# The token mixer's steps moved between the products of the input projection

## The chip, the cores and the metric

One core of one Trainium2 chip runs one program. The metric is the device time of an execution in microseconds (us); the median of three runs is shown. A core has TensorE (PE; its weight loads are PEld), VectorE (DVE), ScalarE (ACT), GpSimd (POOL) and SyncE (SP), each with an instruction queue of its own that runs in order; they wait for each other with semaphores. Sixteen DMA engines move data for all queues.

## The reference

One inference step of a two-layer diffusion backbone for 384 tokens of width 1024, in three tiles of 128: tile 0 is the new context request, tiles 1 and 2 are the 256 latent tokens (a grid of 4 rows x 64). Each layer, cut to what matters:

```python
mod = ada_modulation(cvec, w_ada[l], b_ada[l])            # silu(c) @ w_ada, 6 x 1024 columns
h = rms_norm(x, norm_g[l, 0]) * (1 + sc_m) + sh_m
q, k, v, u, vm, bg, cg, hx = split_projection(h @ w_in)   # 512,512,512,256,256,256,256,256 columns
o_att = attend(q, k, v)          # context: dense softmax; latents: masked window + bias, and cached context keys
vm = rms_norm(gelu(vm), g_v)
o_mlp = gelu(u) * (einsum('hpq,bcqhd->bcphd', w_s, vc) + b_s)      # chunks of 128 tokens
o_conv = bg * sum(pad(cg * hx)[:, j:j + n] * w_conv[:, j] for j in range(3))
y = concatenate([o_att, o_mlp, o_conv]) @ w_out
x = x + gt_m * rms_norm(y, norm_g[l, 1])
# then a second norm with modulation, and SwiGLU: dense in layer 0, top-2 of 8 experts in layer 1
```

## The kernel before

All weights come from memory in chunks of 1 MB (two transfers of 512 KB) through a ring `raw` of six slots, in the order of a table `STREAM`. SP issues chunk n when TensorE has finished chunk n - 6 (`s_pe`). A projection runs in split precision: ScalarE copies a chunk rounded to `whi` (three buffers, line 574), VectorE writes the remainder over the ring slot as `wlo` (line 805), and TensorE makes three products per piece (`three`, lines 1134 to 1136). The helper `upto(n)` stands wherever ScalarE or VectorE should have split the stream up to chunk n; what follows it on that queue waits.

The input projection `win` has eleven chunks per layer: columns in blocks of 512, two chunks (the two halves of the 1024 inputs) per block, in the order q, k, v, u with vm, B with C, and one 256-wide chunk for h. Per chunk and token tile there are 12 products of 512 columns (24 of 256 in the last). Sums stand in PSUM banks 2t + b%2, and ScalarE evacuates them to `pr` (line 713). Modulation weights are not split: TensorE multiplies them raw (`ada`, line 1173, 16 products for a group of two chunks), after each of eight input chunks (`ADA_IN_WIN`) one group; VectorE adds the bias row that POOL loads (`brow`), and for some groups TensorE turns the row into columns (`ada_turn`, line 1158).

Behind the projection stands `mixer`, on each engine as a block of its own: transposes of q, k and the cached keys (lines 1249, 1253), the gating products (1260), row shifts for the convolution as products with a shift matrix (1274), and then twelve units, each a pair of heads of one tile: scores (1291 to 1294), VectorE's scaling, bias and maximum (`soft`, 1016 to 1026), ScalarE's exponential (744), transposes of the weights (1303), ScalarE's copy (753), products with the values (1317), VectorE's division (1033). The convolution (999 to 1004) sits on VectorE between the second and third unit. Last, eight column tiles of `pr` are transposed (1336) and split into `xhi` and `xlo`, and the output projection `wout` (four chunks q) begins. POOL prepares the position bias in two steps: 8 small loads (line 485), one transfer of all rows to memory in a repeated form (`rpb_pad`, line 487), and 16 transfers back (`bias`, line 497).

## Time and profile before

| | us |
|---|---|
| median of three runs (1877.98 to 1895.23) | 1886.65 |
| profiled execution, its own time | 1877.55 |
| its span, first to last instruction | 1875.7 |
| PE busy | 1695.2 (90%) |
| DVE busy | 1093.5 (58%) |
| ACT busy | 928.3 (49%) |
| mean granted TensorE clock | 0.942 |

Busy time of PE is the time in which a product is under way; products are pipelined, so it says little of the rate. The clock is the granted share of full speed, 1.00 for 2.4 GHz and 0.50 for 1.2 GHz. In order of time the program is: start with the first modulation groups and the norm (to 55.6 us), layer 0 with its mixer and dense channel part, layer 1 from about 603 us with its mixer, and the experts from about 905 us to the end.

### The profile page before, as it was taken

To read this page: it belongs to the slowest core of one execution; us is meant where nothing else is said; L and a number is where in the kernel's file an instruction comes from. 1 tells how busy PE (TensorE), PEld (TensorE's weight loads), DVE (VectorE), ACT (ScalarE), POOL (GpSimd) and SP (SyncE) were. 2 spreads that over 40 slices of the span, in tenths; PEclk is the share of its full clock that TensorE was granted. 3 is DMA by queue.
4 is the path that set the end of the run, shared out by engine and by line. 5 is a ranking of instruction groups with operands and counts; after the bars stand their busy time and mean duration, and the time that the engine had idled before them with its cause. 6 is when DMAs were issued, how large, how long until landed. Compare 5 with 4: busy or idle time off the path is not lost.

```text
span 1875.7 us, 20363 instructions
## 1 busy us (share of the span) xinstructions
PE 1695.2 (90%) x7938; PEld 1336.3 (71%) x7938; DVE 1093.5 (58%) x1214; ACT 928.3 (49%) x1137; POOL 177.5 (9%) x189
## 2 busy tenths in 40 slices
PE   4988787999999888788599999999999999999994
PEld 1656675888877656676488788778887777787772
DVE  1423635343323423543399888889888966666653
ACT  2314335332313324245377777777777755545541
POOL 3220000000000230000202011020202020010001
PEclk9998887999999889887699999999999999999996
DMA  9795012343354796002399999999999986566643
GB/s 331 228 318 189 23 46 68 113 135 113 134 213 169 191 307 243 23 24 68 136 356 367 352 376 349 372 350 378 350 381 350 374 261 204 207 222 215 218 160 114
DMA packets 296572, 423.19 MB, mean 226 GB/s; under 512 B 22116, under 2 KB 226944, under 8 KB 296464
## 3 DMA queue, kind: packets, MB, share of 16 engines
q1 hardware_dynamic: 281504, 394.85, 62.1%
q0 software_dynamic: 13952, 24.29, 4.8%
q10 hardware_dynamic: 1008, 2.62, 0.4%
q8 instruction: 67, 1.10, 0.2%
q14 instruction: 41, 0.34, 0.1%
HBM read 418.56 MB, written 21.99 MB: 235 GB/s over the span
## 4 chain that ended last, share of the span: by engine, by line
PE 81%; DVE 6%; DMA 5%; ACT 3%; issue 3%; SPq 1%; POOL 0%; POOLq 0%; DVEq 0%; ACTq 0%
PE ps L1134 22%; PE ps L1136 21%; PE ps L1135 21%; PE ps L1140 3%; PE ps L1141 3%; DMA raw<-in_w_in_dram 2%; PE ps L1173 2%; PE ps L1401 1%; SPq L399 1%; PE ps L1479 1%; DMA raw<-in_w_moe_gu_dram 1%; PE ps L1317 1%; PE ps L1198 1%; PE ps L1158 1%; DMA raw<-in_w_ada_dram 1%
## 5 line engine op out<-in xcount | busy, mean ns | idle before, releaser
L805 DVE TENSOR_TENSOR wlo<-raw,whi 128x2048 fp32r<-128x2048 f32 x327 | 746.8, 2291 | 369.2 <-ACT whi L574 368.6
L574 ACT ACTIVATE whi<-raw 128x2048 fp32r<-128x2048 f32 x327 | 625.9, 1917 | 377.2 <-DMA raw<-in_w_in_dram 122.3
L1134 PE MATMUL ps<-whi,xhi 128*128 128x512 f32 (+1 forms) x1352 | 543.4, 402 | 42.0 <-issue 19.6
L1135 PE MATMUL ps<-wlo,xhi 128*128 128x512 f32 (+1 forms) x1352 | 528.0, 391 | 0.0
L1136 PE MATMUL ps<-whi,xlo 128*128 128x512 f32 (+1 forms) x1352 | 527.9, 390 | 0.0
L1134 PEld LDWEIGHTS ps<-whi,xhi 128*128 128x128 f32 x1352 | 258.9, 192 | 114.3 <-DVE wlo L805 31.0
L1136 PEld LDWEIGHTS ps<-whi,xlo 128*128 128x128 f32 x1352 | 258.2, 191 | 53.9
L1135 PEld LDWEIGHTS ps<-wlo,xhi 128*128 128x128 f32 x1352 | 259.3, 192 | 48.1 <-issue 0.5
L1134 PE MATMUL ps<-whi,hhi 128*128 128x512 f32 x484 | 196.8, 407 | 0.4 <-DVE pg L910 0.4
L1136 PE MATMUL ps<-whi,hlo 128*128 128x512 f32 x484 | 190.2, 393 | 0.0
L1135 PE MATMUL ps<-wlo,hhi 128*128 128x512 f32 x484 | 189.1, 391 | 0.0
L1136 PEld LDWEIGHTS ps<-whi,hlo 128*128 128x128 f32 x484 | 90.9, 188 | 19.9
L1134 PEld LDWEIGHTS ps<-whi,hhi 128*128 128x128 f32 x484 | 91.0, 188 | 19.0 <-DVE pg L910 1.3
L1135 PEld LDWEIGHTS ps<-wlo,hhi 128*128 128x128 f32 x484 | 91.2, 188 | 17.3 <-issue 0.2
L538 POOL DMA_INDIRECT hx<-h_rows,lidx x24 | 49.7, 2069 | 523.0 <-PE ps L1479 431.0
L659 ACT ACTIVATE pg<-ps 128x256 f32<-128x256 f32 x121 | 43.6, 380 | 100.4 <-PE ps L1401 91.2
L908 DVE TENSOR_TENSOR pg<-pg,ps 128x256 f32<-128x256 f32 x121 | 48.5, 416 | 70.7 <-ACT pg L659 60.1
L551 POOL DMA_INDIRECT y_rows<-f,lidx x24 | 45.8, 1910 | 324.7 <-ACT f L698 318.0
L672 ACT ACTIVATE xhi<-ps 128x384 fp32r<-128x384 f32 x64 | 31.4, 491 | 86.0 <-PE ps L1479 85.4
L1140 PE MATMUL ps<-whi,xhi 128*128 128x512 f32 x176 | 68.6, 390 | 2.0 <-DVE xhi L929 2.0
L1173 PE MATMUL ps<-raw,cS 128*32 128x512 f32 x384 | 53.8, 675 | 18.3 <-DMA raw<-in_w_ada_dram 17.5
L1141 PE MATMUL ps<-wlo,xhi 128*128 128x512 f32 x176 | 68.7, 390 | 0.0
(211 smaller groups left out, 1389.0 us busy)
## 6 DMA issues: line engine op xcount, KB each, us to landing
raw<-in_w_moe_gu_dram SPq DMA_DIRECT2D x352, 512.0 KB, 6.0
raw<-in_w_moe_d_dram SPq DMA_DIRECT2D x176, 512.0 KB, 6.2
raw<-in_w_ada_dram SPq DMA_DIRECT2D x96, 512.0 KB, 5.5
raw<-in_w_in_dram SPq DMA_DIRECT2D x44, 512.0 KB, 5.7
raw<-in_w_ffn_gu_dram SPq DMA_DIRECT2D x44, 512.0 KB, 4.3
raw<-in_w_ffn_d_dram SPq DMA_DIRECT2D x22, 512.0 KB, 6.5
raw<-in_w_out_dram SPq DMA_DIRECT2D x16, 512.0 KB, 4.4
rpb_pad<-pad POOLq DMA_DIRECT2D x2, 1778.0 KB, 17.9
```

What stands on the lines that cost most here:

```text
L538: pool.indirect_dma_start(out=hx[:, i, :], out_offset=None, in_=h_rows[:, :], in_offset=bass.IndirectOffsetOnAxis(ap=lidx[:, e, i:i + 1], ...
L551: pool.indirect_dma_start(out=y_rows[:, :], out_offset=bass.IndirectOffsetOnAxis(ap=lidx[:, e, i:i + 1], axis=0), in_=f[:, i, :], in_offse ...
L574: act.activation(whi[m % SPL][:, :], raw[n % RING][:, :], ACT.Copy).then_inc(s_hi, 1)
L659: ins = act.activation(pg[:, t, :], ps[:, 2 * t + b % 2, 0:256], ACT.Silu)
L805: dve.tensor_tensor(wlo[n % RING][:, :], raw[n % RING][:, :], whi[NTH[n] % SPL][:, :].bitcast(F32), ALU.subtract).then_inc(s_lo, 1)
L908: ins = dve.tensor_tensor(pg[:, t, :], pg[:, t, :], ps[:, 2 * t + b % 2, 256:512], ALU.mult)
L1134: pe.matmul(out, a_hi, w_hi, start=start, stop=False)
L1135: pe.matmul(out, a_hi, w_lo, start=False, stop=False)
L1136: return pe.matmul(out, a_lo, w_hi, start=False, stop=stop)
L1140: pe.matmul(out, a, w_hi, start=start, stop=False)
L1141: return pe.matmul(out, a, w_lo, start=False, stop=stop)
L1173: ins = pe.matmul(ps[32 * k:32 * k + 32, 6, :], cS[:, 4 * h + k, :], w[:, k, :], start=(h == 0), stop=(h == 1))
```

## The change

The input chunks come in another order (`WIN_SEQ`): u with vm first, then q, k, v, then h, and B with C last. In the following, position 0 to 10 is a chunk's place in that order, and a slot is one token tile of a chunk, so that a chunk is three slots. The modulation groups stand two together behind positions 2 to 5 (`ADA_AFTER`) instead of one behind each of eight chunks. Each token tile has one PSUM bank (t) for its sums, used by all blocks in turn. The mixer's steps are called from inside `win` on every engine, by tables that name the slot: transposes in positions 5 and 6, scores from position 7 on, a unit's transposes two slots behind its score and its value products three behind. The gating part runs from position 1 to 4. The context units come first and share one value step. The last value step, six of the eight column tiles and the convolution move into `wout`. The row shifts are no longer products: POOL copies z shifted by one row to `zp` and `zn`. POOL also issues its small loads, the bias rows and their detour ahead of the fifth modulation row. Buffers move accordingly.

```diff
-ADA_IN_WIN = {w: HEAD + w - 1 for w in range(1, 1 + ADA_B - HEAD)}
+WIN_SEQ = [6, 7, 0, 1, 2, 3, 4, 5, 10, 8, 9]
+ADA_AFTER = {2 + p: [HEAD + 2 * p, HEAD + 2 * p + 1] for p in range((ADA_B - HEAD) // 2)}
...
-        for w in range(N_WIN):
+        for p, w in enumerate(WIN_SEQ):
             out.append(("win", l, w))
-            if w in ADA_IN_WIN:
-                out += [("ada", l, 2 * ADA_IN_WIN[w] + h) for h in range(2)]
+            for i in ADA_AFTER.get(p, []):
+                out += [("ada", l, 2 * i + h) for h in range(2)]
...
-        UNITS = [(t, h) for t in (1, 2, 0) for h in range(0, NH, 2)]
...
+        UNITS = [(0, h) for h in range(0, NH, 2)] + [(t, h) for h in range(0, NH, 2) for t in (1, 2)]
         NU = len(UNITS)
+        N_OWN = NH // 2
+        QK = [("q", 0), ("q", 1), ("q", 2), ("q", 3), ("c", 0), ("k", 0), ("k", 1), ("k", 2), ("k", 3)]
+        QK_AT = {-3: [0, 1], -2: [2, 3], 0: [4], 1: [5, 6], 2: [7, 8]}
+        SCORE_AT = [3, 3, 4, 4] + list(range(5, 13))
+        OWN_AT = 7
+        MIXED_AT = {13: [0, 1]}
+        MIXED_BANK = [5, 6, 6, 7, 6, 7, 6, 7]
...
+        def slot(p, t):
+            return NT * (p - 6) + t
+        def units_at(j, lag):
+            return [u for u in range(NU) if SCORE_AT[u] + lag == j]
...
@@ POOL
+            def shift_rows(l):
+                pool.wait_ge(s_sc, NU * (l + 1))
...
+                pool.wait_ge(s_z, l + 1)
+                pool.dma_start(zp[1:P, :, :], z[0:P - 1, :, :]).then_inc(s_zs, 16)
+                pool.dma_start(zn[0:P - 1, :, :], z[1:P, :, :]).then_inc(s_zs, 16)
+                pool.wait_ge(s_zs, 64 * l + 32)
+                pool.dma_start(zp[0:1, 2, :], z[P - 1:P, 1, :]).then_inc(s_zs, 16)
+                pool.dma_start(zn[P - 1:P, 1, :], z[0:1, 2, :]).then_inc(s_zs, 16)
...
+                pool.dma_start(ws[:, :, :], w_s[l].rearrange("h p q -> p h q")).then_inc(s_ld[l][1], 16)
+                pool.dma_start(bs[:, :], b_s[l].rearrange("h p -> p h")).then_inc(s_ld[l][2], 16)
+                chain(pool.memset(pad[:, :], NEG))
+                for h in range(NH):
+                    pool.dma_start(pad[7 * h:7 * h + 7, 48:79], rpb[l, h, 4:11, :]).then_inc(s_pad, 16)
+                pool.dma_start(ck[:, :], cache_k[0, l].rearrange("p h d -> p (h d)")).then_inc(s_ld[l][4], 16)
+                pool.dma_start(cv[:, :], cache_v[0, l].rearrange("p h d -> p (h d)")).then_inc(s_ld[l][5], 16)
+                pool.wait_ge(s_pad, (16 * NH + 16) * (l + 1) - 16)
+                pool.dma_start(rpb_pad[l], pad[0:56, :].rearrange("p (a k) -> p a k", a=1).to_broadcast([56, GW, 127])
...
+                pool.dma_start(wcb[:, :, :].rearrange("p c j -> p (c j)"),
...
+                pool.wait_ge(s_tr, KT * (2 * l + 1))
+                clear_brow(l, HEAD)
                 norm_row(l, 1)
                 brow(l, 4)
                 brow(l, 5)
...
@@ ScalarE, in win(l)
+                for p, w in enumerate(WIN_SEQ):
+                    n, b = PLACE["win", l, w], w // 2
+                    last = w % 2 == 1 or w == 10
...
                     for t in range(NT):
...
+                        j = slot(p, t)
+                        if t == 0:
+                            upto(HALVED[NTH[n] + (1 if 1 <= p <= 5 else 2)])
+                        if last:
+                            if t < NT - 1:
+                                act.wait_ge(s_win, 2 * WIN_B * l + 2 * k + t + 1)
+                            else:
+                                act.wait_ge(s_pe, n + 1)
+                            act.activation(pr[:, t, 512 * b:512 * b + width], ps[:, t, 0:width], ACT.Copy
+                                           ).then_inc(s_pr, 1)
+                        for i in QK_AT.get(j, []):
+                            if i % 2 == 0:
+                                turned_qk(l, i)
+                        for u in units_at(j, 2):
+                            pt_copy(l, u)
+                        for kt in MIXED_AT.get(j, []):
+                            mixed(l, kt)
+                        for u in units_at(j, 0):
+                            exp(l, u)
+                    if p == 1:
...
+                        act.activation(pr[:, :, OU:OU + 512], pr[:, :, OU:OU + 512], ACT.Gelu_apprx_tanh
+                                       ).then_inc(s_gel, 1)
+                        act.wait_ge(s_gel, l + 1)
+                        act.wait_ge(s_pad, (16 * NH + 16) * (l + 1))
+                        for t in range(NT):
+                            rms(5 * l + 1, t, pr[:, t, OVM:OVM + D_CM], sq[:, :], D_CM)
...
+                upto(PLACE["wout", l, 2])
+                for kt in (2, 3, 4, 5):
+                    mixed(l, kt)
+                upto(PLACE["wout", l, 3])
+                for kt in (6, 7):
+                    mixed(l, kt)
...
@@ VectorE
+            def win(l):
+                for p, w in enumerate(WIN_SEQ):
+                    n = PLACE["win", l, w]
+                    for t in range(NT):
+                        j = slot(p, t)
+                        for i in QK_AT.get(j, []):
+                            if i % 2 == 1:
+                                turned_qk(l, i)
+                        for u in units_at(j, 0):
+                            if u == N_OWN:
+                                masked_bias(l)
+                            soft(l, u)
+                        if j == OWN_AT:
+                            own_out(l)
+                        for u in units_at(j, 3):
+                            if u >= N_OWN:
+                                out(l, u)
+                        for kt in MIXED_AT.get(j, []):
+                            mixed(l, kt)
+                        if j == 1:
+                            mod_columns(l, 1)
+                        if t == (1 if p > 5 else 0):
+                            upto(HALVED[NTH[n] + (1 if 1 <= p <= 5 else 2)])
+                    if p == 2:
+                        gate_values(l)
+                    if p == 4:
+                        gated_units(l)
+                    for i in ADA_AFTER.get(p, []):
+                        ada(l, i)
+                    if p == 2:
+                        dve.wait_ge(s_wsp, l + 1)
+                        dve.tensor_copy(wsT[:, :, :].rearrange("p a n -> p (a n)"), ps[:, 3, :]).then_inc(s_wst, 1)
                 dve.wait_ge(s_pr, NT * WIN_B * (l + 1))
                 dve.tensor_tensor(z[:, :, :], pr[:, :, OC:OC + D_CV], pr[:, :, OH:OH + D_CV], ALU.mult
                                   ).then_inc(s_z, 1)
...
+                upto(PLACE["wout", l, 2])
+                out(l, NU - 1)
+                for kt in (2, 3, 4, 5):
+                    mixed(l, kt)
+                convolve(l)
+                upto(PLACE["wout", l, 3])
+                for kt in (6, 7):
+                    mixed(l, kt)
...
@@ TensorE
+            def win(l):
+                k = 0
+                for p, w in enumerate(WIN_SEQ):
+                    b, h = (w // 2, w % 2) if w < 10 else (5, 0)
...
+                    n = PLACE["win", l, w]
+                    pe.wait_ge(s_lo, NTH[n] + 1)
...
                     for t in range(NT):
...
+                        if k and h == 0:
+                            pe.wait_ge(s_pr, NT * WIN_B * l + NT * (k - 1) + t + 1)
+                        for i in range(kk):
+                            kt = 4 * h + i
+                            if p < 2 and t == 0:
+                                pe.wait_ge(s_xlo, KT * 2 * l + kt + 1)
...
+                        if t == NT - 1:
+                            pe_done(ins)
+                        elif last:
+                            ins.then_inc(s_win, 1)
+                        j = slot(p, t)
+                        for i in QK_AT.get(j, []):
+                            turn_qk(l, i)
+                        for u in units_at(j, 0):
+                            score(l, u)
+                        for u in units_at(j, 2):
+                            turn_p(l, u)
+                        if j == OWN_AT:
+                            own_value(l)
+                        for u in units_at(j, 3):
+                            if u >= N_OWN:
+                                value(l, u)
+                        for kt in MIXED_AT.get(j, []):
+                            mixed(l, kt)
+                        if j == 0:
+                            ada_turn(l, ADA_B - 1)
+                    k += last
+                    for i in ADA_AFTER.get(p, []):
+                        ada(l, i)
+                    if p == 2:
+                        turn_ws(l)
+                    if p == 3:
+                        mix(l)
...
+                def before(step):
+                    if step == (2, 1):
+                        pe.wait_ge(s_sm, NU * (l + 1))
+                    if step == (0, 0):
+                        pe.wait_ge(s_pr, NT * WIN_B * (l + 1))
+                    if step == (1, 0):
+                        value(l, NU - 1)
                 def between(q):
+                    if q == 0:
+                        for kt in (2, 3, 4, 5):
+                            mixed(l, kt)
+                    if q == 1:
+                        for kt in (6, 7):
+                            mixed(l, kt)
                     if q == 2:
                         pe.wait_ge(s_mlo, KT * (l + 1))
                         gates(2 * l, gate_m)
-                down(NT, xhi, xlo, lambda q: PLACE["wout", l, q], KT, wait, s_y, between)
+                steps = [(2, 1), (0, 0), (0, 1), (1, 0), (1, 1), (2, 0)]
```

VectorE before, the end of the input projection of layer 0 (`wlo` is the split of a chunk, `bias` the mask, `pr` with `gvb` the gate values):

```order
L840 TENSOR_TENSOR stage<-ps,stage 128x512 [waits s_colmm,s_brow1,s_pe]
L958 TENSOR_TENSOR bias<-bias,win_mask 128x3072 [waits s_const,s_ld0_0]
L816 RECIPROCAL rs<-rs 128x1 [waits s_sq,s_ld0_2]
L967 SCALAR_TENSOR_TENSOR pr<-pr,rs,gvb 128x256 [waits s_dv]
...
L967 SCALAR_TENSOR_TENSOR pr<-pr,rs,gvb 128x256 [waits s_dv]
L805 TENSOR_TENSOR wlo_53<-raw,whi 128x2048 [waits s_hi]
L805 TENSOR_TENSOR wlo_54<-raw,whi 128x2048 [waits s_hi]
```

VectorE in the change, positions 4 and 5 of layer 0 (`wlo` the split of the next chunk, `pr<-ps,bs,pr` the gating, `f<-ps,f` a modulation row, `qT` a transposed q):

```order
L868 TENSOR_TENSOR wlo_50<-raw,whi 128x2048 [waits s_hi]
L1095 SCALAR_TENSOR_TENSOR pr<-ps,bs,pr 128x64 [waits s_mix]
L1095 SCALAR_TENSOR_TENSOR pr<-ps,bs,pr 128x64 x11
L905 TENSOR_TENSOR f<-ps,f 128x512 [waits s_colmm,s_brow0,s_pe]
L905 TENSOR_TENSOR f<-ps,f 128x512 [waits s_colmm,s_brow1,s_pe]
L1018 COPY qT<-ps 128x384 [waits s_qk]
L868 TENSOR_TENSOR wlo_49<-raw,whi 128x2048 [waits s_hi]
L1018 COPY qT<-ps 128x384 [waits s_qk]
```

The late splits no longer stand behind mask and gate values; but in position 4 the gating and two modulation rows stand behind a split.

From position 7 on VectorE has the first latent unit's soft behind the split of that position and the mask (`bias`), which stand behind the four context units'.

TensorE in the change, one slot of position 9 (all 12 products, then score, transposes and value step of three different units):

```order
L1251 MATMUL ps<-whi,xhi 128x512
L1252 MATMUL ps<-wlo_52,xhi 128x512
L1253 MATMUL ps<-whi,xlo 128x512
L1383 MATMUL ps<-kT,qT 128x256 [waits s_sm]
L1384 MATMUL ps<-ckT,qT 128x128
L1383 MATMUL ps<-kT,qT 128x256
L1384 MATMUL ps<-ckT,qT 128x128
L1399 MATMUL ps<-ident,f 128x128 [waits s_ptc,s_ex]
L1399 MATMUL ps<-ident,f 128x128 x5
...
L1414 MATMUL ps<-pr,pT 128x64 x2
L1414 MATMUL ps<-cv,pT 128x64
```

Before, these steps stood one behind the other with no projection product between them.

POOL in the change, layer 0, from the fourth modulation row on:

```order
L458 DMA stage<-in_b_ada_dram 2x512 [waits s_modr]
L515 DMA gvb<-in_g_v_dram 128x256
L517 DMA ws<-in_w_s_dram 128x4x128
L518 DMA bs<-in_b_s_dram 128x4x1
L519 MEMSET pad 128x127
L521 DMA pad<-in_rpb_dram 7x31 [waits s_po]
L521 DMA pad<-in_rpb_dram 7x31 x7
L522 DMA ck<-in_cache_k_dram 128x512
L523 DMA cv<-in_cache_v_dram 128x512
L525 DMA rpb_pad<-pad 3584x1x127 [waits s_pad]
L527 DMA wcb<-in_w_conv_dram 128x768
L452 MEMSET f 128x1024 [waits s_tr]
```

Before, the fifth and sixth modulation rows stood ahead of `pad`, and `gvb`, `ck`, `ws`, `cv`, `bs` behind `bias`, and `wcb` behind all rows.

## Rows read from the trace of the kernel before

**Rows 1.** Table of stages (us, busy us and count per engine, clock, DMA share, GB/s):

```profile
55.60:187.80 132.20, 115.48 (x595) 86.45 (x594) 41.10 (x39) 37.25 (x43) 17.93 (x29) 0.94 0.80 250
187.80:258.30 70.50, 51.86 (x345) 44.51 (x344) 42.09 (x99) 28.45 (x74) 0.00 (x0) 0.79 0.05 15
258.30:290.00 31.70, 31.70 (x131) 24.51 (x130) 8.35 (x6) 10.36 (x10) 0.00 (x0) 0.98 0.32 100
624.40:757.70 133.30, 114.72 (x594) 85.88 (x594) 40.49 (x38) 37.09 (x43) 19.73 (x30) 0.92 0.80 249
757.70:828.00 70.30, 51.66 (x345) 44.25 (x343) 41.99 (x98) 28.24 (x74) 0.00 (x0) 0.79 0.05 16
```

**Rows 2.** Chain of waits, layer 0: start us, us, what:

```profile
73.34 1.85 PE ps L1173 x16
...
83.62 1.85 PE ps L1173 x16
...
94.34 14.84 DMA raw<-in_w_in_dram
...
111.14 2.30 DVE wlo L805
...
167.81 9.26 issue
```

**Rows 3.** Timeline of VectorE, layer 0: start us, us, instruction [idle before]:

```profile
168.08 3.35 DVE L958 TENSOR_TENSOR bias<-bias,win_mask 128x3072 f32<-128x3072 f32 x1
...
174.68 6.69 DVE L805 TENSOR_TENSOR wlo<-raw,whi 128x2048 fp32r<-128x2048 f32 x3
...
195.84 2.39 DVE L985 SCALAR_TENSOR_TENSOR pr<-ps,bs,pr 128x64 f32<-128x64 f32 x12 [1.90 <-PE ps L1260]
```

**Rows 4.** Chain of waits, in layer 0's mixer:

```profile
193.18 2.63 PE ps L1260 x24
...
205.81 1.18 DVE pr L1000
...
229.02 0.85 PE ps L1303 x6
229.87 1.29 PE ps L1317 x12
231.16 0.64 PE ps L1293 x4
231.79 0.26 PE ps L1294 x4
232.07 0.69 DVE f L1020
...
233.13 0.97 DVE nm L1025
```

**Rows 5.** Table of stages, other stretches:

```profile
30.00:40.00 10.00, 8.89 (x40) 3.97 (x32) 0.91 (x2) 3.08 (x4) 0.51 (x1) 1.00 1.05 386
...
90.00:110.00 20.00, 16.04 (x86) 10.40 (x84) 3.68 (x3) 3.08 (x5) 12.56 (x20) 0.99 1.05 280
113.50:168.00 54.50, 54.31 (x276) 39.79 (x276) 13.33 (x12) 14.93 (x15) 1.54 (x3) 0.97 0.88 312
661.50:683.00 21.50, 12.30 (x69) 7.51 (x68) 3.89 (x5) 2.51 (x2) 8.79 (x14) 0.84 1.06 269
```

**Rows 6.** Chain of waits, start of the program:

```profile
28.90 12.80 DMA raw<-in_w_in_dram
```

**Rows 7.** Timeline of POOL, layer 0:

```profile
44.00 5.13 POOL L485 DMA_DIRECT2D pad<-in_rpb_dram  x8 [0.29 <-POOL pad L483]
53.10 1.67 POOL L487 DMA_DIRECT2D rpb_pad<-pad  x1 [3.97 <-DMA pad<-in_rpb_dram]
...
88.30 10.61 POOL L497 DMA_DIRECT2D bias<-rpb_pad  x16
```

**Rows 8.** The page's DMA issues: count, KB each, us to landing:

```profile
rpb_pad<-pad POOLq DMA_DIRECT2D x2, 1778.0 KB, 17.9
```

More of the change, by code:

```diff
@@ L440, in _ @@
             chain(pool.memset(ident[:, :], 0.0))
-            chain(pool.memset(shift[:, :, :], 0.0))
             chain(pool.memset(sel[:, :], 0.0))
@@ L1339, in down @@
             def down(T, hi_of, lo_of, place, nk, wait, s_done, between=None, even_banks=None, bank=lambda t: 2 * t,
-                     half=0):
+                     half=0, first=None, before=None):
                 for q in range(nk // 2):
@@ L1347, in down @@
                         (t, h) for t in range(T + half) for h in (1, 0)]
+                    if q == 0 and first is not None:
+                        steps = first
                     for i, (t, h) in enumerate(steps):
+                        if q == 0 and before is not None:
+                            before((t, h))
                         if q == 0 and i == T + half and even_banks is not None:
@@ L1374, in between @@
                         gates(2 * l, gate_m)
-                down(NT, xhi, xlo, lambda q: PLACE["wout", l, q], KT, wait, s_y, between)
+                steps = [(2, 1), (0, 0), (0, 1), (1, 0), (1, 1), (2, 0)]
+                down(NT, xhi, xlo, lambda q: PLACE["wout", l, q], KT, wait, s_y, between, first=steps, before=before)
             def gates(s, gate):
```

533 lines of the change are left out of this document (252 added, 281 removed).

## Prediction, made before the changed kernel was run

> **What bounds the kernel now.** Read first the table of stages [rows 1]. Between 55.6 and 290 us layer 0 runs three stages: eleven input chunks with the modulation products between them (132.2 us), the mixer (70.5) and the output projection (31.7). Layer 1 repeats the first two in 133.3 and 70.3. In the projection stages TensorE is busy 115 of 132 us. In the mixer it is busy 51.9 of 70.5, at a mean granted clock of 0.79, the transfers stand nearly still (15 GB/s) and VectorE works 42 us. So the mixer is bound by the order of its small steps across engines, and its work would fit beside products. The two ends of the projection stage are worse than they look. The chain of waits [rows 2] shows two holes. One is the 14.84 us load that ends at 109.2, whose split on VectorE is at 111.14: TensorE had finished the modulation at about 106. The other is 9.26 us marked "issue" at 167.81. VectorE's timeline [rows 3] tells what it is: bias and mask (3.35 us), then gate values, then at 174.68 the late splits, which TensorE needs for its last chunk.
>
> **The sum, stage by stage.** I count from the first input product (T, 55.6 us in layer 0).
>
> *Chunks.* Two chunks take 17.7 us from a cold start (55.6 to 73.34), one takes 8.4 (75.2 to 83.62), a modulation group 1.85 [rows 2]. Positions 0 to 2 end at T+26. Before, every modulation group (2 MB) stood behind a chunk of its own; now four stretches carry two groups each, so the ring must bring 5 MB (four modulation chunks and one input chunk, 5.24 MB) per 12.1 us of TensorE work (8.4 + 3.7). At the 386 GB/s of the window 30 to 40 us [rows 5] they take 13.6 us, and the next input chunk is the last of the five. With two splits behind it (1.9 and 2.3 us, [rows 2] for the second) it is late. By hand, with six ring slots freed in order: position 3 can start at T+31, is done at T+39.5, and two groups and the gating products (2.63, [rows 4]) bring T+46; its successor's chunk lands at T+42.5 and is split by T+46.7. Position 4 ends at T+55. There the next chunk lands at T+56.3, is split by T+60.5, and behind that split VectorE still has the gating (2.39, [rows 3]) before the modulation row that TensorE's small turn waits for: position 5 starts at T+64.3 instead of T+60. In position 5 ScalarE waits for the following chunk (landing T+71.3) before it evacuates q's first transposes, and TensorE stops after its second tile. Position 6 starts at T+84. Stalls: 1 + 1 + 4 + 6 = 12 us. The old holes, about 7.5 and 9.26, are gone.
>
> *Positions 6 to 10.* A slot is one token tile of a chunk: 12 products, 2.8 us. Position 6 has the last five of the nine transposes of q, k and the cache between its products: T+84 to T+95.7. In position 7 own-block scores come in; masking the bias (3.35, [rows 3]) lies between soft(3) and soft(4) on VectorE, and score(5) needs soft(4), so I charge 3.3 us there: with the own blocks' value step, the second slot of position 8 (position 8 starts at T+107) ends at T+120. Each following slot carries a score (0.64 + 0.26), six transposes (0.85 at worst, 0.7 taken) and a value step (1.29) [rows 4], so 2.8 + 3.0 = 5.8 us. VectorE has in the same slot 0.69 + 0.97, 0.37 for the operation between those two rows, a third of a 2.3 us split and some 0.6 of small work, 3.4 us: hidden, TensorE bounds. Five such slots, then 5.7 and 4.9 for the last two, end the stage at T+160. Total TensorE work put here is some 33 us of the mixer's; the four shift products are dropped (replaced by POOL copies).
> Before: 132.2 + 70.5 = 202.7. After: 160. Gain 42.7 in layer 0; the same in layer 1, 43.6 (133.3 + 70.3), less the clash below.
>
> *Output projection.* It now holds the last value step (1.3), six of eight mixed tiles. Four come in one place as two ping-pong pairs, about 3 us, two more about 0.7; it no longer begins at the low clock (1.2 saved). +3.8 us per layer. The convolution, six VectorE operations like the 1.18 us one [rows 4], runs 6.4 us beside product q1: z is ready about 1.6 us after the last chunk, the shifted copies land by 10 in the likely case, VectorE is free at 12.6, done at 19, and TensorE asks at 20.8. Hidden by 1.8 us.
>
> *POOL's transfers.* The bias table's detour through memory (1778 KB, 17.9 us, [rows 8]), issued at 53.10 in layer 0, 9.1 us after the first of its small loads at 44.00 [rows 7], now starts on them behind the fourth modulation row instead of the sixth, near 23, with some 3 us of other small loads in between; so it goes out at about 35, while TensorE waits for the first two input chunks, whose load is on the chain from 28.90 to 41.7 [rows 6]. Bounds: nothing if it takes no share; the full 17.9 if it goes first. If it takes every second turn, the 5.7 us left of the chunks become 11.4, and 0.4 MB more of small loads add 1: +6.7 us, which I take, since the window with the same POOL traffic (90 to 110, 280 GB/s, with 1.5 MB of bias pieces in it and the table issued over 10.6 us from 88.30 [rows 5, 7]) leaves the weights at most 200 of 386. In layer 1 the table goes out where it did, but the bias pieces now land at T+20 to T+38, where the two-group stretches begin: at half rate for 12 us the ring loses 6 us, all of it on the path. In the old kernel they cost the hole at 109 (and 269 GB/s in 661.5 to 683 [rows 5]), already counted as gone.
>
> Sum: −42.7 + 3.8 + 6.7 in layer 0, −43.6 + 3.8 + 6 in layer 1: −66. The profiled execution took 1877.55 us (span 1875.7), which is the lower end of the three runs (1877.98) and 9 below their median. From it 1811.5; I lean halfway to the median and forecast **1815**.
>
> **Against the rule.** The rows cannot show how a copy of 127 partitions spreads over the transfer engines: no transfer of the old kernel has that shape. The Trainium skill (DMA: Bandwidth & Descriptors, section "Why a DMA increments its semaphore by 16 and not by 1") says that an engine count must divide the partitions, which gives 127 a single engine, and names an exception in which POOL's copies still use all sixteen; no run here shows either yet.
>
> **Rivals.**
> 1. *The ring keeps up* (12 + 18 us of stalls and the late start hidden). For: the old stretches of one group ran without a hole, TensorE busy 54.3 of 54.5 us [rows 5]. Against: 5 MB per 12 us is 433 GB/s, above anything in [rows 5]. −37: 1778. Chance 0.17.
> 2. *The shifted copies do not spread.* 127 rows of 3 KB, 390 KB, over one engine at 386/16 = 24 GB/s take 16.2 us. Then they land near 25 after the last chunk, the convolution ends at 31.5, TensorE has waited since 20.8: +10.7 per layer, 1836. It is the outcome that the Trainium skill's divisor rule above gives. Chance 0.13.
> 3. *Small steps wait for one another.* In-order TensorE meets a soft not yet done. Upper bound one soft (2.0) per slot, 12 slots, two layers: 48; nothing is the lower. Half: +24, 1839. For: the mixer did wait like this. Against: 2.8 us of products now lie between. Chance 0.14.
> 4. *Slower than before: the weights starve.* Four stretches per layer bring 21 MB, in my hand count from T+17.7 to T+71.3, 54 us. Held to 212 GB/s they take 99 us, 45 more per layer: 1905, slower by 1%. It decides at 36 more per layer, 90 us or 233 GB/s, where the time is the old median. The window 661.5 to 683 (269 in all, POOL's part inside) is that bad for 21 us; POOL is silent in most of the new stretches. Chance 0.03.
> That the steps really stand between products is in the order of instructions; no doubt is left there.
>
> **Numbers.** The forecast has 0.5, the rivals 0.17, 0.13, 0.14 and 0.03, and 0.03 is left for what I have not seen. The range runs from rival 1 to rivals 2 and 3 with some of both: 1780 to 1850; stalls double as long as mine are inside it. A measurement of this kernel tells about 1% from no change. Faster by over 1% (below 1868): all but rival 4 and part of the rest, 0.95; within 1% 0.03; slower 0.02.
>
> **What will show it.** Stage from first input product to last: 160 us (layer 0), 166 (layer 1), with holes before positions 4 to 6 named after whi or wlo; slots of 5.8 us after the masked bias and one hole of about 3 there; the first input product at 62 instead of 55.6; no hole before mixed tile 6, or one of 10 us if the copies come over one engine. I am wrong if the slots are longer than 7 us, if the first product starts at 56, or if the mixed tiles wait for the convolution.

## The result and the profile after

| | before | after |
|---|---|---|
| median, beside each other on one chip, 4 runs each | 1890.94 (1877.98 to 1897.2) | 1824.07 (1823.76 to 1831.32) |
| profiled execution, its own time (span) | 1877.55 (1875.7) | 1831.32 (1829.6) |
| mean granted TensorE clock | 0.942 | 0.956 |

The ratio of the runs (of their means, not of the medians) is **0.9664, 95% interval 0.9604 to 0.9724**. Run once more beside the experiments, the changed kernel took 1829.68 us (1826.54 to 1832.31), ratio 0.9668 [0.9619, 0.9717].

The table of stages, after (busy us and instructions per engine, then granted clock, DMA share, GB/s): the input projection with the mixer inside it, cut at position 6, then the output projection, for both layers.

```profile
69.80:158.50 88.70, 79.12 (x409) 56.26 (x409) 27.41 (x43) 22.98 (x32) 16.72 (x27) 0.90 0.73 250
158.50:234.60 76.10, 73.70 (x483) 63.37 (x483) 42.87 (x72) 40.20 (x82) 1.46 (x2) 0.98 0.32 114
234.60:269.80 35.20, 34.36 (x158) 26.89 (x158) 17.97 (x21) 11.83 (x14) 2.07 (x4) 1.00 0.44 136
603.90:700.50 96.60, 79.05 (x410) 56.40 (x409) 27.19 (x43) 22.37 (x31) 19.06 (x29) 0.86 0.85 255
700.50:776.60 76.10, 73.71 (x484) 63.50 (x484) 42.87 (x72) 40.92 (x82) 1.46 (x2) 0.98 0.32 114
```

Against [rows 1]: 202.7 us of projection and mixer became 164.8 in layer 0, and 203.6 became 172.7 in layer 1. Where the mixer's steps stand (the second and fifth row), TensorE is busy 97% of the time. The mixer alone had 51.9 of 70.5. What is left idle is in the first and fourth row, ahead of position 6.

Where layer 0 starts, the chain of waits shows one load of 26.95 us in the place of the 12.80 us of [rows 6]:

```profile
28.87 26.95 DMA raw<-in_w_in_dram
55.85 1.92 ACT whi L610
57.79 2.29 DVE wlo L868
69.78 0.43 PE ps L1251
```

POOL's timeline and the list of transfers (KB each, us to landing) show what runs beside it, and the windows what all transfers together moved:

```profile
33.96 1.67 POOL L525 DMA_DIRECT2D rpb_pad<-pad  x1 [3.63 <-DMA pad<-in_rpb_dram]
rpb_pad<-pad POOLq DMA_DIRECT2D x1, 1778.0 KB, 23.9
40.00:50.00 10.00, 2.38 (x11) 2.21 (x11) 2.89 (x2) 1.39 (x1) 0.00 (x0) 1.00 1.07 209
50.00:60.00 10.00, 0.00 (x0) 0.00 (x0) 2.21 (x2) 1.91 (x1) 0.00 (x0) 1.00 0.96 223
```

The table's transfer to memory goes out at 33.96 and lands 23.9 us later. Beside it the total falls from 384 GB/s (30 to 40 us) to 209, and the second input chunk, split at 41.7 before, is split at 55.85.

TensorE's holes over 2 us in layer 0 until position 6 and in its masked part; the bracket is the idle time before and what ended it:

```profile
116.22 0.80 PE L1251 MATMUL ps<-whi,xhi 128*128 128x512 f32 x1 [2.87 <-DVE wlo L868]
133.64 1.05 PE L1275 MATMUL ps<-sel,f 128*128 128x2 f32 x8 [2.88 <-DVE f L905]
146.39 1.54 PE L1364 MATMUL ps<-ident,pr 128*128 128x128 f32 x6 [3.83 <-ACT qT L745]
186.12 0.97 PE L1383 MATMUL ps<-kT,qT 64*128 64x256 f32 x4 [2.40 <-DVE nm L1049]
```

They stand before position 4, at the small turn before position 5, inside position 5, and at score 5. Behind the last one no hole over 1.5 us is left, and the scores follow each other evenly:

```profile
198.30 0.71 PE L1383 MATMUL ps<-kT,qT 64*128 64x256 f32 x4
204.07 0.71 PE L1383 MATMUL ps<-kT,qT 64*128 64x256 f32 x4
209.84 0.71 PE L1383 MATMUL ps<-kT,qT 64*128 64x256 f32 x4
```

That is 5.77 us a slot. In layer 1 the chain shows the clash of the bias pieces with the weights, which [rows 2] had, in layer 0, as 14.84 us at 94.34. Here the load holds back position 3, behind a hole of 11.40 us that ends at 645.17:

```profile
621.90 18.96 DMA raw<-in_w_in_dram
640.88 1.92 ACT whi L610
642.83 2.30 DVE wlo L868
645.17 0.80 PE ps L1251
...
677.89 2.00 DVE pr L1095 x10
679.89 0.61 DVE f L905
680.54 1.87 PE ps L1275 x8
```

POOL's copies for the convolution (first list: POOL's timeline; second: transfers with KB and us to landing):

```profile
236.56 0.54 POOL L499 DMA_DIRECT2D zp<-z  x1 [12.65 <-DVE z L1151]
zp<-z POOLq DMA_DIRECT2D x1, 381.0 KB, 3.7
zn<-z POOLq DMA_DIRECT2D x1, 381.0 KB, 4.7
254.29 2.28 DVE L868 TENSOR_TENSOR wlo<-raw,whi 128x2048 fp32r<-128x2048 f32 x1
```

They land in under 5 us, VectorE has the convolution behind it at 254.29, and TensorE has no hole before mixed tile 6 (at 254.74).

### The profile page after: what moved, and what is told of

It is laid out like the page before. It is cut to its first block, busy times and chain, and to the rows that moved or that the text cites. A ratio compares the mean times of both kernels' runs of the same rounds, so it can differ in the third digit from the quotient of the medians.

```text
span 1829.6 us, 20275 instructions
## 1 busy us (share of the span) xinstructions
PE 1672.5 (91%) x7906; PEld 1319.1 (72%) x7906; DVE 1088.1 (59%) x1202; ACT 926.6 (51%) x1137; POOL 183.4 (10%) x197
## 4 chain that ended last, share of the span: by engine, by line
PE 81%; DMA 7%; DVE 5%; ACT 3%; issue 2%; SPq 1%; POOL 1%; POOLq 0%; DVEq 0%; ACTq 0%
PE ps L1251 22%; PE ps L1253 21%; PE ps L1252 21%; DMA raw<-in_w_in_dram 4%; PE ps L1257 3%; PE ps L1258 3%; PE ps L1577 2%; PE ps L1293 1%; PE ps L1655 1%; SPq L429 1%; DVE wlo L868 1%; PE ps L1414 1%; DMA raw<-in_w_moe_gu_dram 1%; ACT whi L610 1%; PE ps L1318 1%
```

## The experiments

In the table each layer has two readings of TensorE's timeline: the start of the first product of the input projection, and that of the output projection. Their distance is the stage. All kernels are edits of the changed one, but for e7, which is an edit of the kernel before. The two profiled executions of the changed kernel differ by 3 us in layer 0's stage, so smaller differences between two single traces say nothing. "One run" marks a time that was taken once.

| | time, us | ratio to before | layer 0 | stage | layer 1 | stage |
|---|---|---|---|---|---|---|
| before | 1890.94 | | 55.3 to 258.0 | 202.6 | 624.0 to 828.0 | 204.0 |
| after | 1824.07 | 0.9664 | 69.4 to 234.4 | 164.9 | 603.6 to 776.4 | 172.8 |
| after, again (a0) | 1829.68 | 0.9668 | 73.2 to 234.9 | 161.7 | 604.1 to 777.1 | 173.0 |
| e1 table late | 1812.48 | 0.9599 | 57.2 to 222.1 | 165.0 | 591.2 to 761.0 | 169.8 |
| e2 small loads late | 1821.94, one run | | 65.5 to 228.5 | 163.0 | 597.7 to 770.8 | 173.1 |
| e3 table early | 1823.4 | 0.9656 | 70.9 to 233.8 | 162.9 | 603.1 to 770.1 | 167.1 |
| e4 mask early | 1817.89, one run | | 67.3 to 228.0 | 160.8 | 596.0 to 765.4 | 169.4 |
| e5 spread | 1831.32, one run | | 53.5 to 227.2 | 173.7 | 596.3 to 776.8 | 180.5 |
| e6 order | 1825.29, one run | | 72.3 to 231.8 | 159.5 | 600.7 to 771.1 | 170.4 |
| e7 before, last splits first | 1882.62 | 0.9961 | 55.3 to 251.5 | 196.2 | 617.8 to 823.2 | 205.4 |
| e8 four edits | 1792.25 | 0.9471 | 57.5 to 215.7 | 158.3 | 584.0 to 741.1 | 157.2 |
| e9 four edits, spread | 1801.8 | 0.9526 | 53.7 to 228.7 | 175.0 | 597.0 to 747.1 | 150.1 |
| e10 table in long rows | 1823.35, one run | | 62.2 to 226.8 | 164.6 | 596.0 to 769.0 | 173.0 |
| e11 four edits, spread in layer 1 | 1783.36 | 0.9447 | 57.2 to 210.1 | 153.0 | 578.2 to 728.0 | 149.8 |

### Layer 0's start: the table's transfer (e1, e2, e10)

e1 lets POOL wait, in layer 0, until the second input chunk is split:

```diff
+                if l == 0:
+                    pool.wait_ge(s_hi, 2)
                 pool.wait_ge(s_pad, (16 * NH + 16) * (l + 1) - 16)
                 pool.dma_start(rpb_pad[l], ...).then_inc(s_pad, 16)
```

> Layer 0's position table (1778 KB) goes out only when ScalarE has split the second input chunk. Theory A (the table's transfer holds back the second input chunk): that chunk lands near 42 us as in the old kernel instead of 55.8, the first input product starts at 56 (+-1) instead of 69.8, and the bias pieces, now landing about 24 us after it, cost a few us at position 3 in return; whole gain 8 to 14 us, time 1810 to 1816. Theory B (the small loads ahead of it, or the stream itself, hold it back): first product stays at 66 or later, time unchanged within 3 us.

Measured: theory A, with a ratio of 0.9599 [0.9552, 0.9646] and the first product at 57.2 instead of 69.4. ScalarE's timeline shows the two splits 3.9 us apart, as in the kernel before (37.84 and 41.73) and not 16.4 as in the changed kernel:

```profile
39.66 1.91 ACT L612 ACTIVATE whi<-raw 128x2048 fp32r<-128x2048 f32 x1 [8.39 <-DMA raw<-in_w_in_dram]
43.58 1.91 ACT L612 ACTIVATE whi<-raw 128x2048 fp32r<-128x2048 f32 x1 [2.01 <-DMA raw<-in_w_in_dram]
```

Layer 0's stage did not grow: the bias pieces, though later, are still there in time. e2 sends the table at once and lets only the other small loads (g_v, w_s, b_s, cached keys and values, convolution weights) wait for the same split.

> The counterpart: in layer 0 the table goes out at once, and the other small loads (gating weights, cached keys and values, gate values, convolution weights, 1.3 MB) only behind the second input chunk's split. Theory A: the first input product still starts at 64 us or later, since the table alone delays the chunk. Theory B: it starts at 60 us or earlier.

The first product came at 65.5: of the 12 to 16 us that e1 took away (69.4 and 73.2 in the two executions of the changed kernel against 57.2), the table alone costs 8, going out 2 us sooner than in the changed kernel (31.99 against 33.96). The other loads add 4 to 8 when they go out together with it; by themselves they cost little, since e1 has them early too, all but the convolution weights. e10 asks whether it is the bytes. Layer 0's table transfer takes its 1778 KB from the input weights in memory, in long rows:

```diff
+                if l == 0:
+                    pool.dma_start(rpb_pad[l].rearrange("r g k -> r (g k)"),
+                                   bass.AP(w_in.tensor, w_in[0].offset, [[GW * 127, 56], [1, GW * 127]])
+                                   ).then_inc(s_pad, 16)
```

> The changed kernel, but in layer 0 the table's transfer has its 1778 KB copied from the input weights in long rows (32.5 KB each) instead of from the padded rows in pieces of 508 bytes; layer 0's bias values are therefore not those of the table, and only the start of layer 0 is read. Theory A (the weights beside it suffer from the number of short packets): the second input chunk's split ends by 47 us and the first input product comes at 59 to 62 us instead of 69.8 to 73.2. Theory B (they suffer from the bytes, which share 380 GB/s however they are cut): 1778 KB is 4.7 us of all transfers, so the first product comes 4 to 5 us later than without it (57.5), at 61.5 to 62.5. Theory C (whatever POOL's queue carries gets a fixed half or more until it is done): as in the changed kernel, 68 us or later.

The first product came at 62.2, 5 us behind e1's, and the transfer landed in 10.6 us instead of 23.9 (list of transfers, then ScalarE's timeline):

```profile
rpb_pad<-in_w_in_dram POOLq DMA_DIRECT2D x1, 1778.0 KB, 10.6
45.80 1.91 ACT L616 ACTIVATE whi<-raw 128x2048 fp32r<-128x2048 f32 x1 [15.13 <-DMA raw<-in_w_in_dram]
48.41 1.91 ACT L616 ACTIVATE whi<-raw 128x2048 fp32r<-128x2048 f32 x1 [0.70 <-DMA raw<-in_w_in_dram]
```

Here it is the first chunk that comes late (45.80 instead of 39.66). Theory C is out. The bytes at 380 GB/s are worth 4.8 us, and 62.2 lies where theory B puts it; of theory A's two marks it misses both a little (the second split ends at 50.3, not by 47). But bytes "however they are cut" cannot be all, since the same bytes in short rows cost 12 to 16. So some 5 us of the delay are bytes, and 7 or more are the form: 508 bytes at a time. The edit changes the source from on-chip rows to memory as well, so row length and source are not told apart. The Trainium skill (DMA: Bandwidth & Descriptors, section "Specifications") puts the smallest transfer for full rate at 512 B; the 508 B rows are just under it, and the fall to 209 GB/s agrees with a rule of that kind, though no run here moved rows of 512 B.

### Layer 1: the same table during the dense part (e3)

The pad rows, g_v, b_s, the table's transfer and the convolution weights of layer 1 are issued at the start of the dense part, where transfers are idle:

```diff
+                if l:
+                    chain(pool.memset(pad[:, :], NEG))
+                    ...
+                    pool.wait_ge(s_pad, (16 * NH + 16) * (l + 1) - 16)
+                    pool.dma_start(rpb_pad[l], ...).then_inc(s_pad, 16)
                 brow(l, 2)
                 brow(l, 3)
```

> Layer 1's table, with its gate values, convolution weights and gating bias, goes out at the start of the dense channel part, 300 us earlier; the bias pieces then follow as soon as the residual is done. Theory A (the bias pieces, landing 20 to 38 us after the first product, starve the ring, so that position 3 waits for its chunk until T+41): the pieces are out before T+10, position 3 starts at T+31 or earlier, layer 1's stage takes 163 to 166 us instead of 172.7, whole gain 7 to 10 us. Rival (the modulation groups alone starve it): position 3 still starts after T+38, gain under 3 us. The dense part should not lengthen by more than 1 us.

The stage of layer 1 fell from 172.9 to 167.1 us, less than the 163 to 166 that theory A asked for, but with its mechanism. The bias pieces go out at 606.29 instead of 623.21, while the first three positions run from the full ring, and position 3 starts at 633.02, without the 11.40 us hole that the changed kernel has there. Part of it comes back before position 4, where TensorE now waits for modulation weights:

```profile
646.12 1.38 PE L1308 MATMUL ps<-raw,cS 128*32 128x512 f32 x8 [1.95 <-DMA raw<-in_w_ada_dram]
653.07 0.80 PE L1266 MATMUL ps<-whi,xhi 128*128 128x512 f32 x1 [0.26 <-DVE wlo L883]
```

The time (1823.4) beside the first one of the changed kernel (1824.07) is no gain at all, so the changed kernel was run once more.

> The changed kernel itself once more, beside the others on one chip, since the early-table run (1823.4 us) came out beside its 1824.07 although its trace is shorter by 5.8 us between layer 1's first input product and its output projection. If the early table really gains 5.8 us, this run reads 1827 to 1831 us here (the early-start run, whose only gain is the first product at 57.5 instead of 69.8 us, had 1812.5 on the chip of the other one, and 1812.5 + 12.3 + a little is 1825 to 1829). If the gain is given back elsewhere, it reads 1822 to 1825.

1829.68 lies in the range that stands for a real gain. But the ratios to the kernel before (0.9668 here, 0.9656 for e3, each with an interval of 0.005 to either side) do not tell the two apart. What shows the gain is the stage: 172.8, 173.0, 173.1 and 173.0 us in four traces without this edit (after, a0, e2, e10), 167.1 with it, and what stands before it no longer than it was (369.3 us from layer 0's output projection to layer 1's first product, 369.2 in the changed kernel). The two medians of the same kernel differ by 5.6 us, which is as much as most single edits here are worth.

### The masked bias (e4)

```diff
-                            if u == N_OWN:
-                                masked_bias(l)
...
+                        if j == 2:
+                            masked_bias(l)
```

> The mask (3.3 us on VectorE) moves from between the context units and the first latent unit to the end of position 6. Theory A (score 5 waits for soft 4, which stands behind split and mask): the hole in the first slot of position 8 goes, the stretch from position 6 to the end of the stage takes 73 us instead of 76.1 in both layers, total gain 5 to 7 us. Rival (the split in front of soft 4 alone makes the wait): under 2 us in all.

The hole at score 5 shrank from 2.40 to 0.49 us, and the distance from position 6 to the output projection from 76.1 to 72.95 in both layers, more than the hole. The rest is the clock. In layer 0 the changed kernel is granted less for a moment after the hole in its first profiled execution (hole until 186.12; first row), but not in the second one (hole until 188.21; second and third row). The fourth row is e4:

```profile
185.00:190.00 5.00, 3.88 (x21) 3.57 (x22) 3.18 (x6) 3.90 (x9) 0.00 (x0) 0.66 0.28 105
185.00:190.00 5.00, 2.61 (x23) 2.25 (x23) 3.85 (x7) 1.81 (x5) 0.00 (x0) 1.00 0.33 129
190.00:195.00 5.00, 5.00 (x45) 4.72 (x44) 2.79 (x6) 3.58 (x9) 0.00 (x0) 1.00 0.11 40
180.00:185.00 5.00, 5.00 (x44) 4.71 (x43) 2.75 (x6) 4.33 (x9) 0.00 (x0) 1.00 0.54 211
```

With the dip the stretch is 76.1 us (layer 1 has it in both executions), without it 74.6 (the second execution, and e2 and e3, all in layer 0), without the hole 72.95.

### Order behind the splits (e6)

```diff
-                        if t == 0:
+                        if t == (2 if p == 5 else 0):
                             upto(...)            # ScalarE's split
...
+                    if p == 4:
+                        gated_units(l)           # ahead of the token tiles
-                        if t == (1 if p > 5 else 0):
+                        if t == (1 if p >= 5 else 0):
                             upto(...)            # VectorE's split
...
-                    if p == 4:
-                        gated_units(l)
```

> Two steps are put elsewhere in VectorE's and ScalarE's order: the gating products (12 of 0.2 us, L1095) ahead of the split of position 4 instead of behind it, and in position 5 the split behind the turns (ScalarE at the third tile, VectorE at the second). Theory A (each hole is a step of TensorE waiting for a copy that stands behind a split whose weights come late): the 2.88 us hole at 133.6 and the 3.83 us hole at 146.4 go, and the stretch from layer 0's first input product to its output projection is 5 to 6.5 us shorter than the 164.8. Theory B (the weights' arrival sets the pace of positions 4 to 6 and the holes are only where the wait shows): the holes go and come back before the first product of position 6, the stretch is 164 to 165 us, and the time is within 1 us of the changed kernel's.

Both holes went, and one came back at the turn behind position 5:

```profile
134.93 1.05 PE L1275 MATMUL ps<-sel,f 128*128 128x2 f32 x8 [0.50 <-DVE f L905]
153.50 1.87 PE L1275 MATMUL ps<-sel,f 128*128 128x2 f32 x8 [3.16 <-DVE f L905]
```

The stage is 159.5 us, 2.2 to 5.4 under the changed kernel's; theory A holds for the first hole and half holds for the second. The single time (1825.29) shows nothing, with a first product at 72.3.

### How much was order alone: the old kernel with its last splits first (e7)

```diff
+                upto(PLACE["win", l, N_WIN - 1])
                 mod_columns(l, 1)
 
                 dve.wait_ge(s_ld[l][0], 16 * 2 * NH)
```

> The kernel before the change, with one step moved: in VectorE's order the split of the last input chunks (L868 of the changed kernel's numbering) stands ahead of the modulation columns, the mask addition and the gate values, which it stood behind. Theory A (the 9.26 us in which TensorE issued nothing between the projection and the mixer of the old kernel was this order, and the rest of the gain is overlap): 17 to 18.5 us faster than the old kernel for two layers, ratio about 0.991, so that under a third of the 61 us gain needs no overlap at all. Theory B (the hole would be filled by another wait, such as the bias pieces): ratio 0.996 to 1.0. Theory C (overlap was worth little and order was the most of it): ratio below 0.98.

Ratio 0.9961 [0.9932, 0.9991]: 4.6 us between the medians, 7 by the ratio. That is neither theory A nor C; it lies in theory B's range. The 9.26 us are gone in both layers, but the mixer behind them grew. Its windows with e7, from its first transposes to the output projection:

```profile
176.90:251.50 74.60, 53.19 (x346) 45.62 (x345) 45.92 (x100) 30.00 (x77) 0.00 (x0) 0.78 0.05 15
742.90:823.20 80.30, 59.88 (x346) 52.07 (x346) 46.20 (x100) 29.89 (x77) 0.00 (x0) 0.70 0.05 14
```

[rows 1] had 70.5 and 70.3 us at 0.79. In each layer 3.3 us of the growth are another wait, as theory B said, though not for the bias pieces: TensorE's first transposes now wait for the copies of q, and VectorE's stand behind two splits (layer 1):

```profile
745.48 0.55 PE L1254 MATMUL ps<-ident,pr 128*128 128x128 f32 x3 [1.27 <-ACT qT L736]
748.07 2.16 PE L1254 MATMUL ps<-ident,pr 128*128 128x128 f32 x9 [2.05 <-DVE qT L977]
```

The rest is the clock, in layer 1 above all. The end of that mixer before (first two rows) and with e7 (third):

```profile
795.00:815.00 20.00, 16.58 (x142) 15.06 (x142) 12.43 (x35) 10.54 (x31) 0.00 (x0) 1.00 0.01 2
815.00:830.00 15.00, 11.29 (x45) 9.15 (x46) 6.36 (x17) 6.95 (x16) 0.23 (x1) 0.54 0.00 0
795.00:825.00 30.00, 25.57 (x115) 22.34 (x116) 11.36 (x34) 12.06 (x34) 0.03 (x1) 0.54 0.00 1
```

After a stretch of small steps the granted clock was 0.54, and in e7's mixer, which started 14.6 us earlier, it was so for twice as long. Of some 60 us, this one change of order brings 5 to 7. It is not all that order could bring: the old mixer has one more large hole, behind the convolution on VectorE (layer 0; 7.69 us in layer 1), which the change moves away too and which no run took alone.

```profile
211.21 1.54 PE L1303 MATMUL ps<-ident,f 128*128 128x128 f32 x6 [7.70 <-DVE pr L1004]
```

Even with both holes of both layers taken at their full length, 34 us, a good part of the gain is left to the overlap, with the clock that comes with it: 0.79 in the old mixer, 0.98 where its steps stand now.

### Together (e8), and the modulation products spread (e5, e9, e11)

e8 is e1, e3, e4 and e6 in one kernel.

> Four edits together on the changed kernel: layer 0's table transfer waits for the split of the second input chunk, layer 1's table is built and written during the dense part, the mask addition stands three slots earlier, and the two steps of the order experiment. If the single gains add up: 12.3 (first product earlier) + 5.8 (layer 1's positions 3 to 5) + 2 x 3.1 (mask) = 24.3 us from the changed kernel, so 1799 to 1802 us, with another 5 to 10 us if the order experiment's theory A holds (1790 to 1796). If they overlap, because a weight transfer takes the place of each wait that is removed, 1805 to 1812.

1792.25 us, ratio 0.9471 [0.9434, 0.9508]: the gains add up, with the order experiment's share (1790 to 1796). e5 changes one line of the changed kernel:

```diff
-ADA_AFTER = {2 + p: [HEAD + 2 * p, HEAD + 2 * p + 1] for p in range((ADA_B - HEAD) // 2)}
+ADA_AFTER = {0: [4], 1: [5], 2: [6], 3: [7], 4: [8, 9], 5: [10, 11]}
```

> The changed kernel with the modulation products spread over positions 0 to 5 (pieces 4, 5, 6, 7, then 8 and 9, 10 and 11) instead of two pieces behind each of positions 2 to 5. Theory A (two pieces in a row empty the ring of weights, and the split behind them is late: the 2.9 us before position 4 and the holes before position 6): the distance from layer 0's first input product to position 6 falls from 87 to 89 us to about 83, and the same in layer 1, where positions 3 and 4 start 4 to 8 us sooner. Theory B (the bytes between the first product and position 6 are the same 22 MB and the transfers run without a gap, so the pace is theirs): no difference beyond 1 us at position 6. Theory C (pieces 4 and 5 now come while the table and the bias pieces use the transfers): the holes move to positions 1 and 2, and layer 1 is slower by 3 us or more.

The first product no longer has a second split ahead of it and comes at 53.5, but position 1 then waits 8.42 us, and layer 1's stage grows by 8 us: theory C, with a gain in layer 0 (its output projection begins 7 us sooner) that cancels it. e9 is e8 with the same line.

> The four edits together (1792.25 us, ratio 0.9471) with the spread modulation products as well. If the spread helps as its theory A says, where the table is out of the way it takes 2 to 4 us from each layer's distance to position 6 (81.8 and 83.1 us in the four-edit run): 1785 to 1789 us, ratio about 0.944. If the pace is the bytes', 1791 to 1794 us. If it takes the first chunks' transfers, 1795 us or more.

1801.8 us, slower than e8. Its layers part: layer 1, with no table transfer beside it, has the stage down from 157.2 to 150.1; in layer 0 the table meets the third chunk:

```profile
88.62 0.80 PE L1267 MATMUL ps<-whi,xhi 128*128 128x512 f32 x1 [13.19 <-DVE wlo L884]
```

e11 spreads them in layer 1 alone.

> The four edits together, and the modulation products spread over positions 0 to 5 in layer 1 alone. In layer 1 the run that spread both layers (with the table written during the dense part) had 150.1 us from the first input product to the output projection, against 157.2 of the four-edit run; in layer 0, where the table has to be written beside the first chunks, its output projection began 13 us later, with 13.19 us of waiting at 88.6. Theory A (the spread pays where no table transfer takes the ring's share, and costs where one does): layer 0 as in the four-edit run (output projection at about 215.7), layer 1 150 us, 7 us from the 1792.25: about 1785 us, ratio 0.943 to 0.945. Theory B (layer 1's gain in that run came from what layer 0's delay changed, not from the spread): 1790 to 1794 us.

**1783.36 us, ratio 0.9447 [0.9416, 0.9478]**: theory A, and the best of all, 2.2 to 2.5% under the changed kernel (1824.07 and 1829.68). Its two stages:

```profile
57.20:210.10 152.90, 146.25 (x892) 114.30 (x890) 70.38 (x115) 63.26 (x114) 18.18 (x29) 0.99 0.63 208
577.90:728.00 150.10, 147.53 (x893) 114.56 (x893) 73.11 (x117) 65.39 (x115) 18.09 (x29) 0.98 0.60 205
```

TensorE is busy 147.5 of 150.1 us in layer 1, so little is left there but its own work. Layer 0 gained 5 us on e8 although nothing in it was changed: the granted clock was higher, 0.98 against 0.95 up to position 6 (80.0 against 83.0 us) and 1.00 against 0.97 behind it (72.9 against 75.2). Why is not shown. So only the 7 us of layer 1's stage are the edit's; the 9 us between the medians hold more than that, and the two ratios' intervals overlap.

## Why the prediction was right, and where it was off

The forecast was 1815 us in a range of 1780 to 1850; 1824.07 lies in it, 9 us above the forecast.

Against the profile of before: start 55.6 us, stages 202.7 and 203.6, output projection 31.7.

| term | predicted | measured |
|---|---|---|
| layer 0's first product later | 6.7 | 14.2 |
| layer 0, first product to output projection | 160 | 164.8 |
| layer 1, the same | 166 | 172.7 |
| output projection, each layer | +3.8 | +3.5 |
| sum | −66 | −47.6 |

From 1877.55 the measured terms give 1830.0, and the profiled execution took 1831.32, so nothing of size is missing from the list.

**The chunks' sum held as far as the order of work sets it.** Position 6 to the output projection was counted as 76 us and measured 76.1, in both layers; slots 5.8 and 5.77; the stall of the mask 3.3, measured 2.40. The 1.5 us that complete the 76.1 are the clock's dip, which was not in the count. The turn before position 5 came at T+64 as counted, behind the split and the gating products on VectorE, and e6 shows that this was the cause. The inside of position 5 was under-counted: position 6 started at T+88.7, not T+84, though the stall in it was 3.83 us and not 6. The granted clock behind the holes explains most of it, where the forecast had counted all work at the full one:

```profile
134.60:158.30 23.70, 19.87 (x97) 13.77 (x98) 4.79 (x5) 4.92 (x7) 0.37 (x1) 0.78 0.54 191
```

If all of these 19.87 busy us went with the clock, 0.78 of them, 15.5, would be left at 1.00: an estimate of up to 4.4 us.

**The mis-sized term is the table's transfer.** "If it takes every second turn" gave 6.7 us. It took more: the first product came 14.2 us later, of which e1 shows at least 12 to be the table's transfer and the convolution weights behind it. Equal turns would mean equal bytes; e10 shows that bytes alone would have cost 5. The bounds (nothing to 17.9) held it, but the value within them was taken from the wrong window. The prediction says that POOL issued the table over 10.6 us from 88.30; by [rows 7] those are the 16 bias pieces, and the table had gone out at 53.10. The old kernel's window with the table's own transfer in it was this one:

```profile
60.00:70.00 10.00, 10.00 (x45) 8.26 (x44) 0.74 (x1) 0.60 (x1) 0.00 (x0) 1.00 0.85 147
```

The DMA engines were busy for 0.85 of it and moved 147 GB/s; at 0.80 they moved 250 in [rows 1]. That was a sign that this transfer takes more of them than its bytes say.

**Layer 1's clash** was 6 us over layer 0's stage in the forecast and 8 measured (172.7 against 164.8), with a hole of 11.40 us before position 3, where the bias pieces were said to meet the weights. e3 takes 5.8 of it away.

**The base.** The profile of before is one of its quickest executions: 1875.7 us of span at a clock of 0.942, while its others run up to a span of 1898.6 at 0.926 to 0.932. Those of the changed kernel lie within 1822.0 to 1830.6, at 0.944 to 0.960. So the medians differ by 57 to 67 us in the two comparisons, and the two profiles by 46. The profiled execution of the changed kernel is the slowest of its four. With the terms as measured (−47.6), the base that leads to 1824.07 is 1871.7; the forecast used 1881.1, so that its step of 3.5 us toward the old median went the wrong way. The terms were 18.4 us too good and the base 9.4 too high, and that the forecast is off by only 9 us is luck to that extent; so is it that its gain of 66 matches the 67 between the medians. Why executions of the old kernel are granted less clock was not tried; that the old mixer runs at 0.79 and the new stretch at 0.98 is a candidate.

**Rivals.** The ring kept up (rival 1): no, holes of 2.9 to 11.4 us before positions 3 to 5 and inside 5. Copies on one engine (rival 2): no; 127 rows of 3 KB landed in 3.7 and 4.7 us, against 16.2 for one engine at 24 GB/s. By the Trainium skill (DMA: Bandwidth & Descriptors, section "Why a DMA increments its semaphore by 16 and not by 1") this is the exception that it names for some of POOL's direct copies, not its divisor rule; the trace agrees with the exception. Small steps waiting for one another (rival 3): only at score 5. Starving (rival 4): no, from the first product to position 6 the transfers ran at 250 and 255 GB/s on average.

## What to carry to other kernels

A chain of small steps is hidden by giving each of them a slot between products, and it pays twice, since the clock stays up (0.98 instead of 0.79). Taking only the hole in front of it brought little: e7 gained 5 to 7 us for two holes of 9.26, because another wait and the clock took the rest back. Before moving a load earlier, look at what it meets there: the table moved to where the first weights come in cost 12 us, in the dense part next to nothing, and one wait put ahead of it gave them back. Spreading the modulation products in both layers lost 9 us (e9 against e8), although it won 7 in layer 1's stage (e9 and e11), so try such an edit stage by stage, and read stages rather than totals while two medians of one kernel differ by 5 us. And look up which transfer a window really holds before taking a rate from it.

## What the runs showed of the hardware

- A transfer of 1778 KB in rows of 508 bytes on POOL's queue beside the weights took 23.9 us and held the sum of all transfers at 209 to 223 GB/s; the same bytes in long rows from memory landed in 10.6 us and delayed the weights by 5 us instead of 12 or more. Its source differs too.
- A hole of 2.40 us in an otherwise busy stretch was followed in one execution, in layer 0, by a window of 0.66 granted clock, in another by none; the stretch was 1.5 us longer with it. In layer 1 both executions had the dip (0.74 and 0.71).
- The old mixer, started 14.6 us earlier in layer 1, was granted 0.54 for 30 us at its end, where before it was 1.00 and then 0.54 for 15, and it took 80.3 us instead of 70.3, of which 3.3 are new waits.
